# The head of two feed-forwards: first weights on ACT's queue and split in halves by VectorE, token sums and spread moved inside later blocks, Silu's table loaded ahead

## What is computed

```python
def rms_norm(x, g):
    xf = x.astype(jnp.float32)
    y = xf * lax.rsqrt(jnp.mean(xf * xf, axis=-1, keepdims=True) + RMS_EPS)
    return y.astype(x.dtype) * g

def swiglu(h, w_in, w_out):
    gate, up = _split_last(h @ w_in, (D_FF, D_FF))
    return (jax.nn.silu(gate) * up) @ w_out

x = x + 0.5 * swiglu(rms_norm(x, ffn1_norm[l]), ffn1_w_in[l], ffn1_w_out[l])
...
x = x + 0.5 * swiglu(rms_norm(x, ffn2_norm[l]), ffn2_w_in[l], ffn2_w_out[l])
```

## Time and profile before

| | us |
|---|---|
| median of 3 runs (2692.25 to 2694.45) | 2693.38 |
| the profiled execution | 2693.66 |
| its span, first to last instruction | 2691.9 |
| TensorE busy in it | 2530.2 |
| mean granted TensorE clock | 0.977 |

### The profile page before, as it was taken

The page is one execution under the profiler, slowest core; times in us unless marked ns, Lnnn a source line. Parts: engine busy times, 40 slices in busy tenths (PEclk is TensorE's granted clock), DMA queues, the critical chain, the costliest instruction groups (busy, mean ns, idle before and its releaser), DMA issues.

```text
span 2691.9 us, 50605 instructions
## 1 busy us (share of the span) xinstructions
PE 2530.2 (94%) x19738; PEld 2036.3 (76%) x19738; DVE 1262.7 (47%) x2016; ACT 1053.6 (39%) x1848; POOL 805.7 (30%) x342
## 2 busy tenths in 40 slices
PE   7999999999999999898999999989988989888997
PEld 6888886878787887776777887878776668666676
DVE  3222234444444538345242222236765774575775
ACT  4222234333433434554333222233336652335662
POOL 3444443323232333212433444422221002223002
PEclk9999999999999999998999999999999999999999
DMA  4333332222222222111332333321110002122002
GB/s 138 93 93 94 101 102 83 81 71 75 69 74 78 69 82 80 48 40 55 105 118 89 95 94 97 101 63 55 47 55 25 1 2 62 41 65 75 17 2 70
DMA packets 52009, 188.53 MB, mean 70 GB/s; under 512 B 5760, under 2 KB 6016, under 8 KB 51712
## 3 DMA queue, kind: packets, MB, share of 16 engines
q1 hardware_dynamic: 50688, 181.74, 22.1%
q10 hardware_dynamic: 1152, 4.26, 0.5%
HBM read 183.88 MB, written 2.10 MB: 69 GB/s over the span
## 4 chain that ended last, share of the span: by engine, by line
issue 72%; POOL 14%; PE 11%; DVE 2%; ACT 1%; POOLq 1%; DMA 0%; DVEq 0%; SPq 0%; ACTq 0%
POOL WLO L2604 14%; PE psum L312 2%; PE psum L314 2%; PE psum L313 2%; PE psum L2365 1%; PE psum L2344 1%; PE psum L2380 1%; PE psum L2350 0%; DVE MX L2435 0%; DVE RN L2068 0%; POOLq L2601 0%; ACT PX L2402 0%; DMA RAW<-in_wstream 0%; PE psum L2181 0%; POOLq L2603 0%
## 5 line engine op out<-in xcount | busy, mean ns | idle before, releaser
L2604 POOL TENSOR_TENSOR WLO<-RAW,WHI 128x1024 fp32r<-128x1024 f32 x334 | 800.7, 2398 | 1858.4 <-ACT WHI L300 1858.2
L300 ACT ACTIVATE WHI<-RAW 128x1024 fp32r<-128x1024 f32 x336 | 355.8, 1059 | 1120.2 <-PE psum L314 809.9
L312 PE MATMUL psum<-HHI,WHI 128*128 128x512 f32 x848 | 339.9, 401 | 17.9 <-DVE HLO L484 11.5
L313 PE MATMUL psum<-HLO,WHI 128*128 128x512 f32 x848 | 336.3, 397 | 0.0
L314 PE MATMUL psum<-HHI,WLO 128*128 128x512 f32 x848 | 336.0, 396 | 0.0
L312 PE MATMUL psum<-H2HI,WHI 128*128 128x512 f32 (+1 forms) x536 | 199.8, 373 | 23.7 <-DVE CIN L2103 9.5
L312 PEld LDWEIGHTS psum<-HHI,WHI 128*128 128x128 f32 x848 | 160.0, 189 | 59.6 <-issue 12.5
L313 PE MATMUL psum<-H2LO,WHI 128*128 128x512 f32 (+1 forms) x536 | 192.8, 360 | 0.0
L314 PE MATMUL psum<-H2HI,WLO 128*128 128x512 f32 (+1 forms) x536 | 192.5, 359 | 0.0
L313 PEld LDWEIGHTS psum<-HLO,WHI 128*128 128x128 f32 x848 | 160.1, 189 | 39.2 <-issue 1.2
L314 PEld LDWEIGHTS psum<-HHI,WLO 128*128 128x128 f32 x848 | 160.0, 189 | 39.0
(11 more groups left out here) (421 smaller groups left out, 5026.3 us busy)
## 6 DMA issues: line engine op xcount, KB each, us to landing
RAW<-in_wstream SPq DMA_DIRECT2D x336, 512.0 KB, 3.6
X<-in_xT SPq DMA_DIRECT2D x8, 256.0 KB, 6.8
out_T<-OUT SPq DMA_DIRECT2D x4, 512.0 KB, 2.7
W3S<-in_lora ACTq DMA_DIRECT2D x5, 384.0 KB, 3.2
XC<-in_ctxT ACTq DMA_DIRECT2D x1, 1024.0 KB, 7.1
TRIG<-in_trig ACTq DMA_DIRECT2D x1, 960.0 KB, 9.1
FCC<-in_first SPq DMA_DIRECT2D x1, 576.0 KB, 8.4
LVL<-in_levels SPq DMA_DIRECT2D x1, 384.0 KB, 8.8
```

Of the source, the lines that this page charges most:

```text
L300: act.activation(WHI[:, q % 2, :], RAW[:, q % 2, :], ACT.Copy).then_inc(rounded, 1)
L312: pe.matmul(out, tile_of(WHI, slot, u), hi(kt), start=first and last[0], stop=False)
L313: pe.matmul(out, tile_of(WHI, slot, u), lo(kt), start=False, stop=False)
L2604: pool.tensor_tensor(WLO[:, s, :], RAW[:, s, :], WHI[:, s, :].bitcast(F32), ALU.subtract)\
```

## The change

- Weights block 0 is fetched by ACT's DMA queue, as ACT's first instruction, and no more by SP.
- Block 0 is rounded in two halves by ACT and split in two halves by VectorE, before and after the first HLO; TensorE waits for the second half at tile 4. POOL's first split is that of block 1.
- In ffn1 ACT's wait for the end of b0 and the rounding of b2 move from behind the eight squares to between the fourth and the fifth.
- In both feed-forwards the token sums move from between b1 and b2 into b2, ahead of its tile 4, and the spread from between b2 and b3 into b3, ahead of its tile 2.
- A Silu of one column, and so its table, stands right behind the root, ahead of b3's rounding; the Sqrt dummy has one column instead of two.

```diff
             def first_ready(t):
 
                 pe.wait_ge(*pre.dve.at(f"lo{t}"))
-            block_ready(pe, st.b0)
+                if t == KT // 2 and not f.updates:
+                    block_ready(pe, st.b0)
+            if f.updates:
+                block_ready(pe, st.b0)
...
+            def small(q, t):
+                if (q, t) == (2, KT // 2):
+                    pe.wait_ge(*pre.act.at("copied"))
+                    token_sums(pe, TOKENS, bank[5], [SUMF]).then_inc(*pre.pe.inc("sum"))
+                if (q, t) == (3, 2):
+                    pe.wait_ge(*pre.dve.at("root"))
+                    spread_roots(pe, TOKENS).then_inc(*pre.pe.inc("spread"))
             for q in range(1, 4):
                 block_ready(pe, st.b0 + q)
                 product(pe, bank[q], (st.b0 + q) % 2, [(u, u) for u in range(KT)], lambda t: HHI[:, t, :],
-                        lambda t: HLO[:, t, :], WHOLE).then_inc(k.blocks_used, 1)
-                if q == 1:
-                    pe.wait_ge(*pre.act.at("copied"))
-                    token_sums(pe, TOKENS, bank[5], [SUMF]).then_inc(*pre.pe.inc("sum"))
-                if q == 2:
-                    pe.wait_ge(*pre.dve.at("root"))
-                    spread_roots(pe, TOKENS).then_inc(*pre.pe.inc("spread"))
+                        lambda t: HLO[:, t, :], WHOLE, lambda t, q=q: small(q, t)).then_inc(k.blocks_used, 1)
...
-            block_out(act, st.b0)
-            round_block(act, st.b0 + 2)
+            if f.updates:
+                block_out(act, st.b0)
+                round_block(act, st.b0 + 2)
             act.wait_ge(*pre.dve.at(f"add{KT - 1}"))
             act.activation(SUMF[:, :], bank[6], ACT.Copy).then_inc(*pre.act.inc("copied"))
-            act.activation(ROOTN[:, 2 * KB:], EPS[:, 0:2], ACT.Sqrt).then_inc(*pre.act.inc("table"))
+            act.activation(ROOTN[:, 2 * KB:2 * KB + 1], EPS[:, 0:1], ACT.Sqrt).then_inc(*pre.act.inc("table"))
             act.wait_ge(*pre.pe.at("sum"))
             token_roots(act, TOKENS, bank[5]).then_inc(*pre.act.inc("std"))
+            act.activation(ROOTN[:, 2 * KB + 1:], EPS[:, 0:1], ACT.Silu).then_inc(*pre.act.inc("gate table"))
             round_block(act, st.b0 + 3)
             act.wait_ge(*pre.pe.at("spread"))
             act.activation(FRSTD[:, :], bank[7], ACT.Copy).then_inc(*pre.act.inc("rstd"))
...
             sp.dma_start(X[:, 0, :], xT[:, 0, :]).then_inc(x_in[0], 16)
-            sp.dma_start(RAW[:, 0, :], wstream[0]).then_inc(raw_full[0], 16)
...
-            for s in range(2):
-                pool.wait_ge(rounded, s + 1)
-                pool.tensor_tensor(WLO[:, s, :], RAW[:, s, :], WHI[:, s, :].bitcast(F32), ALU.subtract).then_inc(split, 1)
+            pool.wait_ge(split, 1)
+            pool.wait_ge(rounded, 2)
+            pool.tensor_tensor(WLO[:, 1, :], RAW[:, 1, :], WHI[:, 1, :].bitcast(F32), ALU.subtract).then_inc(split, 1)
...
         def _(act):
+            act.dma_start(RAW[:, 0, :], wstream[0]).then_inc(raw_full[0], 16)
...
-            round_block(act, 0)
+            act.wait_ge(raw_full[0], 16)
+            act.activation(WHI[:, 0, first_half], RAW[:, 0, first_half], ACT.Copy).then_inc(*cond.act.inc("half"))
             for t in range(KT):
                 gained_scalar(act, ffn1, t)
+                if t == 0:
+                    act.activation(WHI[:, 0, second_half], RAW[:, 0, second_half], ACT.Copy).then_inc(rounded, 1)
                 if t == KT // 2:
                     round_block(act, 1)
             for t in range(KT):
+                if t == KT // 2:
+                    block_out(act, ffn1.up.b0)
+                    round_block(act, ffn1.up.b0 + 2)
                 squared_scalar(act, ffn1, t)
...
+            dve.wait_ge(*cond.act.at("half"))
+            dve.tensor_tensor(WLO[:, 0, first_half], RAW[:, 0, first_half], WHI[:, 0, first_half].bitcast(F32), ALU.subtract).then_inc(*cond.dve.inc("half"))
             for t in range(KT):
                 gained_vector(dve, ffn1, t)
+                if t == 0:
+                    dve.wait_ge(rounded, 1)
+                    dve.tensor_tensor(WLO[:, 0, second_half], RAW[:, 0, second_half], WHI[:, 0, second_half].bitcast(F32), ALU.subtract).then_inc(split, 1)
```

More of the change, by code:

```diff
@@ L432, in __init__ @@
                 names = lambda *kinds: [f"{n}{t}" for t in range(KT) for n in kinds]
-                self.pre = Stage(k, KT if updates else 0, ("sum", "spread"), (names("hi", "sq") if updates else names("hi") + names("sq")) + ["copied", "table", "std", "rstd"],
+                self.pre = Stage(k, KT if updates else 0, ("sum", "spread"), (names("hi", "sq") if updates else names("hi") + names("sq")) + ["copied", "table", "std", "gate table", "rstd"],
                                  (names("x", "lo", "add") if updates else names("lo") + names("add")) + ["root"])
@@ L2551, in final_vector @@
                                          op0=ALU.mult, op1=ALU.mult).then_inc(*st.dve.inc(f"out{t}"))
-        cond = Stage(k, 0, (), ("silu", "hi"), ("lo",))
+        cond = Stage(k, 0, (), ("silu", "hi", "half"), ("lo", "half"))
+        first_half = slice(0, UNITS // 2 * P)
+        second_half = slice(UNITS // 2 * P, UNITS * P)
         ffn1 = FFN("ffn1_norm", False)
```

## The result

| | median, us | executions | against the kernel before |
|---|---|---|---|
| before | 2692.87 | 20 (2682.13 to 2697.26) | |
| changed | 2699.38 | 20 (2692.94 to 2706.42) | 1.0029, 95% interval 1.0020 to 1.0038 |

So the change costs 0.29%, 7.8 us by the ratio, 6.5 us between the medians. The forecast was 2702.3, 8.6 us more than the profiled execution of before. The profiled execution of the changed kernel took 2697.23 us, with a span of 2695.4.

What follows compares the result with a forecast made beforehand. The prediction took TensorE's order of work, busy 94% of the span, as the bound. It summed 2693.66 − 0.45 (start) + 6.8 (heads) + 2.3 (clock) = 2702.3 us, range 2697.5 to 2706.0.

Steps and rivals of the forecast that it cites:

- Main term, the heads: Both feed-forward heads: b3 waits 2.5 us, b4 starts 18.62 us after b1's end; +3.6 and +3.2, together +6.8 us.
- The gain from the table: Path from spread to b4: removing Silu's 1.28 us table load wins only 0.36 us, the rest being covered by VectorE.
- Start: First 20 us: TensorE begins near 8.7, then idles before the sixth HLO; second block's transfer sooner, gain 0.45 us.
- a bound of 1.4: Start: upper bound of the gain in us, if a second queue fills the early microseconds; lower bound 0.
- a sign that the forecast is wrong: Start: b0 ending more than 1.4 us sooner than before would show the forecast wrong.
- the smaller loss that I had tied to it: Whole kernel, given that sign: a start gain of up to 2.8 us counts against a much smaller loss.
- Clock: TensorE's idles at start and heads: three low stretches in five idles against one before, +2.3 us, bounds −1.55 and +5.
- The clock holds: Rival, all TensorE idles: they come, but the clock stays high; 2698.5 to 2700 us, chance 0.17.
- Faster: Rival, start and heads: b3 on time, sixth HLO not held by POOL, clock no longer falls; 2691.0 us, chance 0.07.
- The first transfer doesn't do what it says: Rival, start: weights on ACT's queue delay x, first HLOs and second block, 0 to 1 us later; 2704.5, chance 0.12.
- A pause behind each table load: Rival, heads ahead of b3's rounding: two more pauses of at most 1.4 us; 2705.1 us, chance 0.04.

Runs made afterwards that it cites:

- 5: Changed kernel with ACT's rounding of b3 put ahead of its wait for the sums; 1.0008 against the kernel before.
- 4: Changed kernel with Silu's table moved from in front of b3's rounding to behind it; 1.0006 against the kernel before.
- 6: Changed kernel with the spread back between b2 and b3, sums still inside b2; 0.9980 against the kernel before.
- 3: Two queue runs: kernel before with only the first weights' transfer on ACT's queue, 0.9997; changed kernel with it back on SP's, 1.0026; both against before.
- 2: Changed kernel with the old heads, so only the new start, timed twice; 1.0009, then 1.0008 against the kernel before.
- sp_queue: Changed kernel with the first weights' transfer back on SP's queue, halves kept; 1.0026 against the kernel before.
- heads_only: Kernel before with the new heads of both feed-forwards and the old start; 1.0032 against the kernel before.
- start_only_again: Second timing of the changed kernel with the old heads, so only the new start; 1.0008 against the kernel before.
- act_queue: Kernel before with only the first weights' transfer on ACT's queue, rounding and POOL's split as before; 0.9997 against the kernel before.
- b3_ahead: The run of 5: changed kernel with b3's rounding ahead of ACT's wait for the sums; 1.0008 against the kernel before.
- spread_back: The run of 6: changed kernel with the spread back between b2 and b3; 0.9980 against the kernel before.
- both_ahead: Changed kernel with b3's rounding ahead of the sums and b4's ahead of FRSTD; 2683.75 us against 2692.18, ratio 0.9971.
- 7: b4's rounding ahead of FRSTD: on the kernel before 0.9985, with the new start added 0.9982, on the changed kernel with b3's rounding ahead 0.9971, against before.
- 8: both_ahead with all of x fetched and all HHI made before the second weights block is fetched and rounded; 0.9974 against the kernel before.
- start_only: First timing of the changed kernel with the old heads, so only the new start; 1.0009 against the kernel before.
- x_first: The run of 8: both_ahead with all of x ahead of the second weights block; 0.9974 against the kernel before.

## Why the prediction was right

**Main term, the heads: right to a tenth.** Forecast 18.62 us from b1's end to b4; ffn2 shows 18.62. That the hundredths agree is luck: the way to b3 was 0.08 shorter than reckoned (8.99 for 9.07), b3's two tiles 0.10 longer (1.50 for 1.40), the rest 0.02 shorter. ffn1 shows 19.51 (23.44 to 42.95), 0.86 of it the spread at the low clock (1.91 for 1.05). Each part has a run of its own: the rounding behind sums and table (5 takes 2.6 us off), the table's share (4 takes 1.5 off), the spread's place (6 takes 3.9 off). The parts don't add up to the whole, since each run ends on what is late next. The gain from the table was 0.36, as worked out.

**Start: chain right, size wrong.** I took 0.45 us for the second block's transfer with a bound of 1.4; b1 began at 17.84 instead of 19.34, 1.50 sooner, past the bound, and past the 1.4 us that I had named as a sign that the forecast is wrong. It was not followed by the smaller loss that I had tied to it: the heads lost what was forecast. Two premises failed. I called the rate the same, and over 9 us it was 263 GB/s instead of 235, some 0.6 us; I called the bytes ahead the same, and they were 0.39 MB fewer, some 0.9 us (3). TensorE's start, said 8.7, was 8.19, and what it then waited for was the constants (SQC), which I had not looked at. In the times no gain from the start is seen, and a gain of this size lies outside both intervals of 2, so the −1.50 below is a figure of one trace.

**Clock: right in number.** Three low stretches in five idles were taken and three came. That is one execution, and the count differs: in sp_queue, with the same heads and the same five idles, two came (b3 in ffn1, b4 in ffn2), in heads_only three in the heads' four. I had all five idles longer than today's; that before the sixth HLO was 1.34 us in the records, not 2.5, and shorter than the 1.86 before b4 today. Against before the three cost 0.86 + 1.55 in ffn1 and nothing in ffn2, where both traces have one: 2.4 us for the 2.3 forecast. The risk at the idle before the sixth HLO is real too: start_only_again pays 1.3 us for it.

**The sum.** In the traces: −1.50 for the start, +3.19 and +3.62 for the two heads at full clock, +2.4 for the low stretches, 7.7 us; the forecast had −0.45, 6.8 and +2.3, 8.65. The ratio says 7.8 (5.4 to 10.2). The one term that was off, the start by 1.05 us, is smaller than the interval, so the times alone could not have shown it; only the trace does. The medians say 6.5, and the start's gain is not in the times of 2, so the nearness of 7.7 and 7.8 is in part chance.

**Rivals.** "The clock holds" didn't happen here. It is not ruled out for other executions: in act_queue it held behind both idles before b4, 1.86 us each, and in b3_ahead behind the one in ffn1 (2.88) but not in ffn2. In spread_back and both_ahead, where those idles are gone, no low stretch came in the heads. "Faster" needed b3 on time and a free sixth HLO. With b3 on time alone (b3_ahead) the kernel is level with before; it gains where the idle before b4 goes as well, by the spread back between the blocks (6) or by b4's rounding ahead (7), and a free sixth HLO added nothing in time (8). "The first transfer doesn't do what it says" is refuted in place (3), though its first step, a delay of x, is real for tile 0. "A pause behind each table load" as well: 1412.00 + 1.28 to the dummy at 1413.30 leaves 0.02 us. The Trainium skill, "ScalarE: Activation LUTs", "What ACT_TABLE_LOAD costs", gives 2.66 us for a switch; the measured 1.30 decides here.

## What to carry to other kernels

When a wait on one engine moves later, list what is queued behind it on that engine and what those instructions feed: here a rounding that needs nothing of the sums stood behind the wait for them, and TensorE began b3 2.5 us late. Taking a table load off a path is worth only what it stuck out beyond the work beside it (0.36 of 1.28 us). Put work that needs only an early event (b4's rounding, b2's end) ahead of the wait for a late one on that engine: this was worth 0.15% on the old kernel, and b3's and b4's roundings moved so turned the changed kernel from 0.29% slower into 0.29% faster.

## What the runs showed of the hardware

- With a second DMA queue for the first weights the DMA engines moved 263 instead of 235 GB/s over the first 9 us: less in the first three (51 against 102), more in the next two (347 and 385 against 207 and 238). The second block was rounded at 11.26 to 11.60 in the traces with two queues and the same order, at 12.05 to 13.14 with one.
- Stretches at 1.2 GHz stood behind idles of TensorE of 1.8 to 2.9 us, but not behind all of them. In the trace of before the idles ahead of b4 are alike in both feed-forwards, 1.86 in the records (ffn2 in the earlier trace rows), and only the one of ffn2 brought a stretch. In act_queue neither did. The same program ran the sixth HLO's place at full clock in start_only and at 0.55 in start_only_again. The idle of ffn1 in before, then the two of act_queue:

```profile
40.42 0.50 PE L312 MATMUL psum<-HHI,WHI 128*128 128x512 f32 x1 [1.86 <-POOL WLO L2604]
```

```profile
38.72 0.50 PE L312 MATMUL psum<-HHI,WHI 128*128 128x512 f32 x1 [1.86 <-POOL WLO L2603]
...
1415.56 0.50 PE L312 MATMUL psum<-HHI,WHI 128*128 128x512 f32 x1 [1.86 <-POOL WLO L2603]
```

- The scatter in untouched work, 1354 to 1362 us for the same stretch at a mean granted clock of 0.98 to 0.99, is as large as the whole effect of the change.
- A VectorE instruction with two inputs in SBUF that started beside a POOL split ended 0.55 us after it (17.07 and 16.52) and took 2.36 us against 0.74; all eight took 0.75 when the split came behind them (x_first).
